# Two-block transformer kernel: first half of the gated features turned during the last read-out, last output units and router by tokens, activation tables loaded ahead

## What is computed

```python
def mlstm_readout(h, z, x_c, ml_norm, ml_skip):          # 4 heads of 256 features
    hf = h.transpose(0, 2, 1, 3)
    hn = hf * lax.rsqrt(jnp.mean(hf * hf, axis=-1, keepdims=True) + EPS)
    hn = hn.reshape(B, T, ML_INNER).astype(z.dtype) * ml_norm
    return jax.nn.sigmoid(z) * (hn + ml_skip * x_c)

def merge(y_mla, y_ml, g_mla, g_ml, w_out):
    return (jax.nn.sigmoid(g_mla) * y_mla + jax.nn.sigmoid(g_ml) * y_ml) @ w_out

def ec_moe(x, w_router, w_e_gate, w_e_up, w_e_down):     # 16 experts, 32 tokens each
    aff = jax.nn.softmax((x @ w_router).astype(jnp.float32), axis=-1)
    g, idx = lax.top_k(aff.transpose(0, 2, 1), cap)
    xs = jax.vmap(lambda xb, ib: xb[ib])(x, idx)
    a = jnp.einsum('becd,edf->becf', xs, w_e_gate)
    u = jnp.einsum('becd,edf->becf', xs, w_e_up)
    y = jnp.einsum('becf,efd->becd', jax.nn.silu(a) * u, w_e_down) * g[..., None].astype(x.dtype)
...
        x = x + g1[:, None, :] * out_l                    # out_l is what merge gives
        h_l = modulate(rmsnorm(x, norm2[l]), sh2, sc2)
        x = x + g2[:, None, :] * ec_moe(h_l, w_router[l], w_e_gate[l], w_e_up[l], w_e_down[l])
    return rmsnorm(x, final_norm)
```

## Time and profile before

| | us |
|---|---|
| runs: lowest, median, highest | 1703.22, 1708.28, 1709.57 |
| profiled execution: time | 1701.2 |
| profiled execution: span of the core | 1699.4 |
| busy in the span: PE, ACT, DVE, POOL | 1511.7, 525.2, 489.6, 601.3 |

### The profile page before, as it was taken

The page is one execution under the profiler, slowest core; times in us unless marked ns, Lnnn a source line. Parts: engine busy times, 40 slices in busy tenths (PEclk is TensorE's granted clock), DMA queues, the critical chain, the costliest instruction groups (busy, mean ns, idle before and its releaser), DMA issues.

```text
span 1699.4 us, 17483 instructions
## 1 busy us (share of the span) xinstructions
PE 1511.7 (89%) x7424; PEld 1010.9 (59%) x7424; DVE 489.6 (29%) x803; ACT 525.2 (31%) x683; POOL 601.3 (35%) x167
## 2 busy tenths in 40 slices
PE   5999999999999999999999999989887676676756
PEld 4776678877777658887788886657642131131111
DVE  2222333331222232332244346567410000000001
ACT  5255353433425524434344434254210000000000
POOL 4655187734655517774447671010000000000000
PEclk9999999999999999999999999889898898998898
DMA  6533355598453435569725443000799999999996
GB/s 239 185 124 125 124 176 179 183 334 292 157 178 111 147 125 175 177 198 380 252 91 174 149 138 96 1 15 1 299 405 423 421 421 421 422 421 422 422 422 285
DMA packets 125496, 395.38 MB, mean 233 GB/s; under 512 B 6743, under 2 KB 10644, under 8 KB 101228
## 3 DMA queue, kind: packets, MB, share of 16 engines
q1 hardware_dynamic: 123536, 388.66, 61.6%
q0 software_dynamic: 1456, 4.52, 0.7%
q10 hardware_dynamic: 428, 1.10, 0.2%
HBM read 393.19 MB, written 1.05 MB: 232 GB/s over the span
## 4 chain that ended last, share of the span: by engine, by line
PE 70%; DMA 23%; DVE 2%; ACT 2%; issue 1%; SPq 1%; ACTq 0%; DVEq 0%
PE psum L1960 16%; PE psum L1962 16%; PE psum L1961 16%; DMA ring<-in_w_e_down 6%; DMA arena<-in_w_e_gate 5%; DMA ring<-in_w_e_up 4%; PE psum L1952 4%; PE psum L1056 4%; DMA arena<-in_w_e_down 3%; DMA ring<-in_w_in 2%; DMA hT<-in_w_e_up 2%; DMA arena<-in_w_e_up 2%; PE psum L2191 1%; PE psum L973 1%; PE psum L844 1%
## 5 line engine op out<-in xcount | busy, mean ns | idle before, releaser
L593 POOL TENSOR_TENSOR ring_lo<-ring,ring_hi 128x2048 fp32r<-128x2048 f32 x101 | 467.8, 4636 | 362.2 <-ACT ring_hi L574 362.2
L1960 PE MATMUL psum<-ring_hi,hT_lo 128*128 128x512 f32 (+2 forms) x912 | 366.5, 402 | 16.1 <-DVE hT_lo L2209 10.6
L1962 PE MATMUL psum<-ring_hi,hT_hi 128*128 128x512 f32 (+2 forms) x912 | 356.8, 391 | 0.0
L1961 PE MATMUL psum<-ring_lo,hT_hi 128*128 128x512 f32 (+2 forms) x912 | 354.5, 389 | 0.0
L574 ACT ACTIVATE ring_hi<-ring 128x2048 fp32r<-128x2048 f32 x116 | 222.1, 1915 | 385.4 <-DMA ring<-in_w_in 123.0
L1056 PE MATMUL psum<-arena 128*32 128x512 f32 x740 | 169.6, 678 | 57.0 <-DMA arena<-in_w_e_gate 21.2
L1960 PEld LDWEIGHTS psum<-ring_hi,hT_lo 128*128 128x128 f32 x912 | 172.4, 189 | 58.6 <-issue 12.2
L1056 PE MATMUL psum<-ring,arena 128*32 128x512 f32 x708 | 156.6, 664 | 56.0 <-DMA ring<-in_w_e_down 19.9
L1962 PEld LDWEIGHTS psum<-ring_hi,hT_hi 128*128 128x128 f32 x912 | 172.1, 189 | 38.2
L1961 PEld LDWEIGHTS psum<-ring_lo,hT_hi 128*128 128x128 f32 x912 | 173.0, 190 | 33.9 <-issue 0.5
L1056 PEld LDWEIGHTS psum<-arena 128*32 128x32 f32 x740 | 36.0, 121 | 161.7 <-issue 55.9
(11 more groups left out here) (390 smaller groups left out, 1644.3 us busy)
## 6 DMA issues: line engine op xcount, KB each, us to landing
ring<-in_w_in SPq DMA_DIRECT2D x60, 1024.0 KB, 5.2
ring<-in_w_up SPq DMA_DIRECT2D x32, 1024.0 KB, 5.6
ring<-in_w_down SPq DMA_DIRECT2D x32, 1024.0 KB, 5.8
arena<-in_w_e_gate SPq DMA_DIRECT2D x31, 1024.0 KB, 26.7
arena<-in_w_e_up SPq DMA_DIRECT2D x31, 1024.0 KB, 27.0
ring<-in_w_e_gate SPq DMA_DIRECT2D x30, 1024.0 KB, 26.7
ring<-in_w_e_up SPq DMA_DIRECT2D x29, 1024.0 KB, 27.0
ring<-in_w_e_down SPq DMA_DIRECT2D x29, 1024.0 KB, 27.0
```

Source lines behind the costliest of these rows:

```text
L593: eng.tensor_tensor(slot_lo(u), slot(u), slot_hi(u).bitcast(F32), ALU.subtract).then_inc(done, 1)
L1960: pe.matmul(dst, lo(k0 + k), w_hi, start=start and k == 0, stop=False)
L1961: pe.matmul(dst, hi(k0 + k), w_lo, start=False, stop=False)
L1962: last = pe.matmul(dst, hi(k0 + k), w_hi, start=False, stop=stop and k == nk - 1)
```

## The change

All of it lies in the last part of the mixer and in the router.

- Heads are normed in pairs. `head_means` for heads 0 and 1 stands in `weights(3)`, their Sqrt (with `root_soon`, an activation of one column that loads the table) behind ACT's last decays, `head_gates` for them ahead of head 2's denominators, `head_sums` and the low half ahead of head 3's denominators. Heads 2 and 3 follow head 3's features.
- PE turns features 0 to 511 between the two tiles of head 3's read-out, and the second half between the two tiles of `out_unit(1, 0)`. The low half of the first goes to a tile of its own, `gatedT_lo`, since the decays and values of head 3 are still in use where it lay.
- The last two output units run by token tiles: (tile 0, columns 0), (tile 0, columns 1), (tile 1, columns 0), turning of x for tile 0, (tile 1, columns 1). The third unit's slot comes back after three quarters of this, the fourth's at its end.
- The router's logits are made for each tile of tokens by eight matmuls of 16 columns, 128 x 128 features each; part sums, their copy and the two summing matmuls are gone. `lg_full` 2 now says that the logits are done.
- `exp_ahead`, an activation of one column, loads the Exp table behind the root of the means; ACT's two scalings of x move behind the router's Exp. The first MAX8 and MATCH_REPLACE8 read PSUM, and the copy ahead of them is gone.

```diff
@@ PE
+                    if h == MH - 1 and t == 1:
+                        pe.wait_ge(mix_v, 8)
+                        turn_gated(0, 0)
...
-            pe.wait_ge(mix_v, 10)
-            turn_gated(0, 0)
+            def gated_rest():
+                pe.wait_ge(mix_v, 16)
+                turn_gated(1, 3)
+
             pe.wait_ge(gb_sb, 1)
             pe.wait_ge(turn_lo, 18 * DEPTH + 1)
             out_unit(0, 0)
-            pe.wait_ge(mix_v, 16)
-            turn_gated(1, 3)
-            out_unit(1, 0)
+            pe.wait_ge(h_v, 8 * MH)
+            out_unit(1, 0, gated_rest)
+            router_bias()
             pe.wait_ge(turn_lo, 18 * DEPTH + 2)
-            router_bias()
-            out_unit(0, 1)
-            out_unit(1, 1)
...
+            def turn_token(t, db):
+                for half in range(2):
+                    for k in range(4 * half, 4 * half + 4):
+                        last = pe.transpose(flat[db][:, k * P:(k + 1) * P], eighths(x[:, t, :], k), ident)
+                    last.then_inc(turn_full, 1)
+
+            def logits(t, half):
+                for k in range(4 * half, 4 * half + 4):
+                    last = pe.matmul(psum[:, t, 0:NE], hT[:, k, t * P:(t + 1) * P], wr[:, k, 0:NE], start=k == 0, stop=k == KC - 1)
+                return last
+
+            for t, n in ((0, 0), (0, 1), (1, 0), (1, 1)):
+                u = U_OUT + 2 + n
+                if t == 0:
+                    unit_ready(u)
+                if t and n:
+                    pe.wait_ge(x2_v, 4)
+                    pe.wait_ge(rt_v, 2)
+                    turn_token(0, 0)
+                last = split_product(DB[1 + n][:, t, :], tokens(hT_hi, t), tokens(hT_lo, t), UC, u, start=False, stop=True)
+                last.then_inc(slots_free if t else o2_half, 1)
+
+            pe.wait_ge(turn_a, TURN_A + 10)
+            logits(0, 0)
+            logits(0, 1)
+            pe.wait_ge(x2_v, 8)
+            turn_token(1, 3)
+            pe.wait_ge(turn_a, TURN_A + 11)
+            logits(1, 0)
+            pe.wait_ge(turn_v, TURN_V + 10)
+            logits(1, 1).then_inc(lg_full, 1)
@@ DVE
                 low_out(h)
+                if h == MH - 1:
+                    head_means(slice(0, 4), 4)
                 dve.wait_ge(raw_full, 2 * h + 2)
...
+                if h == MH - 2:
+                    head_gates(0, 5, 2)
                 if h == MH - 1:
-                    head_out(0, 3, 0, 6)
+                    head_sums(0, 6)
+                    dve.wait_ge(turn_a, TURN_A + 9)
+                    low_gated(0, flat[0])
                 dve.wait_ge(num_full, h + 1)
...
-            dve.wait_ge(lg_full, 4)
-            top_step(dve.tensor_copy(affT, psum[0:NE, 0, 0:T]))
+            dve.wait_ge(lg_full, 3)
             for r in range(CAP // 8):
                 eight = slice(8 * r, 8 * r + 8)
-                top_step(dve.max(top[:, eight], affT))
-                top_step(dve.match_replace(affT, top[:, eight], affT, -1.0))
+                left = affT if r else psum[0:NE, 0, 0:T]
+                top_step(dve.max(top[:, eight], left))
+                top_step(dve.match_replace(affT, top[:, eight], left, -1.0))
@@ ACT
                 if h == MH - 1:
+                    act.activation(root_soon, amp1[:, 0, 0:1], ACT.Sqrt).then_inc(at_sb, 1)
+                    act.wait_ge(mix_v, 1)
+                    act.activation(hst[:, 2, 0:4], hst[:, 1, 0:4], ACT.Sqrt).then_inc(hn_a, 1)
                     act.wait_ge(gb_full, 1)
...
             act.activation(half_r, means2, ACT.Sqrt).then_inc(norm_a, 1)
+            act.activation(exp_ahead, amp1[:, 0, 0:1], ACT.Exp).then_inc(at_sb, 1)
+            act.wait_ge(rt_v, 5)
+            for t in range(TT):
+                act.activation(aff[:, t, :], aff[:, t, :], ACT.Exp, bias=rst[:, 0, t:t + 1],
+                               accum_out=rst[:, 1, t:t + 1]).then_inc(rt_a, 1)
             act.wait_ge(norm_v, NORM_V + 3)
             for t in range(TT):
                 act.activation(xn[:, t, :], x[:, t, :], ACT.Copy, scale=r_sq[:, t:t + 1]).then_inc(norm_a, 1)
-            act.wait_ge(rt_v, 6)
```

More of the change, by code:

```diff
@@ L425, in build @@
         aff = piece(612, TT, NE)
-        root_ahead, table_ahead = piece(692, 1), piece(693, 1)
+        root_ahead, table_ahead, exp_ahead, root_soon = [piece(692 + i, 1) for i in range(4)]
         rst = piece(644, 4, TT)
@@ L952, in spread, with turn_gated @@
                 last.then_inc(gb_full, 1)
+            def turn_gated(half, db):
+                for k in range(4):
+                    for t in range(TT):
+                        c = 4 * half + k
+                        last = pe.transpose(flat[db][:, k * T + t * P:k * T + (t + 1) * P], gated[:, t, c * P:(c + 1) * P], ident)
+                last.then_inc(turn_full, 1)
             for h in range(MH):
@@ L975, in tensor_block2, with out_unit @@
                 last.then_inc(num_full, 1)
[L977 to L984, removed]
+            def out_unit(n, kh, between=None):
                 u = U_OUT + 2 * kh + n
@@ L987, in out_unit @@
                 for t in range(TT):
-                    last = split_product(DB[1 + n][:, t, :], tokens(hT_hi, t), tokens(hT_lo, t), UC * kh, u, start=kh == 0, stop=kh == 1)
+                    if t == 1 and between:
+                        between()
+                    last = split_product(DB[1 + n][:, t, :], tokens(hT_hi, t), tokens((gatedT_lo, hT_lo)[kh], t), UC * kh, u, start=kh == 0, stop=kh == 1)
                     if n == 1 and kh == 1 and t == 0:
@@ L1021, in tensor_block2 @@
-            pe.wait_ge(rt_v, 2)
-            for half in range(2):
-                if half == 0:
-                    pe.wait_ge(turn_v, TURN_V + 10)
-                else:
-                    pe.wait_ge(turn_a, TURN_A + 10)
-                for j in range(4):
-                    k = 4 * half + j
-                    last = pe.matmul(psum[32 * j:32 * j + 32, 0, 0:T], wr[:, k, :], hT[:, k, :], start=half == 0, stop=half == 1)
-            last.then_inc(lg_full, 1)
-            pe.wait_ge(rt_v, 3)
@@ L1032, in tensor_block2 @@
-            for t in range(TT):
-                last = pe.matmul(psum[:, 1, t * NE:(t + 1) * NE], part_sums[:, t * P:(t + 1) * P], const("sum16"), start=True, stop=True)
-            last.then_inc(lg_full, 1)
-            pe.wait_ge(rt_v, 9)
+            def turn_token(t, db):
+                for half in range(2):
+                    for k in range(4 * half, 4 * half + 4):
+                        last = pe.transpose(flat[db][:, k * P:(k + 1) * P], eighths(x[:, t, :], k), ident)
+                    last.then_inc(turn_full, 1)
@@ L1764, in scalar_block2 @@
                     squares_of(act, h - 1)
-            act.wait_ge(mix_v, 1)
-            act.activation(hst[:, 2, 0:6], hst[:, 1, 0:6], ACT.Sqrt).then_inc(hn_a, 1)
             act.wait_ge(turn_full, FULL + 5)
@@ L1783, in scalar_block2 @@
                 act.activation(xn[:, t, :], x[:, t, :], ACT.Copy, scale=r_sq[:, t:t + 1]).then_inc(norm_a, 1)
-            act.wait_ge(rt_v, 6)
-            for t in range(TT):
-                act.activation(aff[:, t, :], aff[:, t, :], ACT.Exp, bias=rst[:, 0, t:t + 1],
-                               accum_out=rst[:, 1, t:t + 1]).then_inc(rt_a, 1)
             act.wait_ge(gb_full, 2)
```

110 lines of the change are left out of this document (55 added, 55 removed).

## The result

| | us |
|---|---|
| changed kernel: lowest, median, highest of 11 | 1690.49, 1693.16, 1700.35 |
| kernel before: lowest, median, highest of 11 | 1702.53, 1706.84, 1710.68 |
| ratio, 95% interval | 0.9937 (0.9924 to 0.9951) |
| changed kernel, profiled execution: time, span | 1697.58, 1695.8 |

The change makes the kernel 0.63% faster, 10.7 us, with 8.4 to 13.0 as the interval; the two medians of the table lie further apart, 13.7.

The account below looks back on a forecast made before the run. The expert weight stream, limited only by DMA, was taken to bound the end: min(7.0 + 1.67, 8.9) = 8.67, less 0.2 for the dent, 8.5 us off the median 1708.28, giving 1699.8 us, range 1693.0 to 1704.5.

Parts of the forecast that it names:

- Two moments: Start of the expert weight stream: the end moves by the smaller of A's shift + 1.67 and B's shift.
- B: First issue into a slot that an expert round has given back, at 1244.33 us in the kernel before.
- A: First issue of an expert unit, when out_unit(0,0) gives its slots back, at 1200.48 us in the kernel before.
- A's shift: First expert issue from 1200.48 to 1193.5: 7.0 us earlier, 4.3 from waits and 2.7 from the clock.
- The margins: Slack at new waits: 0.85 us and 0.7 us in head 3's read-out, 0.6 us in out_unit(1,0).
- Rival 2: New waits on DVE bite and the clock falls at the output matmuls: gain 4 to 6 us, 1703.3; chance 0.12.
- rival 4: TensorE stays at 1.2 GHz through the output stage, making the kernel slower: 1718 us; chance 0.03.
- The Exp table: Router: table loaded ahead behind the root of the means, Exp at 1218.85, 8.6 us earlier.
- B's shift: First issue into a freed expert slot 8.9 us earlier: 8.6 from Exp, plus 0.45, less 0.1.
- A + 1.67: Gain allowed by the first expert issue: 7.0 plus 1.67 us lost in the stream's dent, 8.67, taken as binding.
- rival 1: B binds: a first expert round at the lower clock costs up to 1.9 us more, time 1701.3; chance 0.2.
- no window under 400 GB/s: Sign expected in the next profile: no such slow window of the expert stream around 1236 us.

Follow-up runs that it names:

- e4: Changed kernel, but the first four expert units (and units 8 and 9) wait for the second output unit, not the first; ratio to the kernel before 0.9973.
- e10: Changed kernel plus unread matmuls behind the gate row's spreading, the turning of the places and the first gathering; ratio to the kernel before 0.9937.
- e3: Kernel before plus output units by tokens, new logits, Exp table ahead and top-8 from PSUM, heads as before; ratio to the kernel before 0.9985.
- e6: Changed kernel plus five unread matmuls, two behind the logits and three behind the gate row's spreading; ratio to the kernel before 0.9948.
- e7: Changed kernel with the first two expert units issued when the last raw scores are done, into other slots; ratio to the kernel before 0.9943.
- e5: Changed kernel without the one-column Exp that loads the table ahead, ScalarE's order kept; ratio to the kernel before 0.9947.
- e9: Changed kernel without the one-column Exp and with ScalarE's two scalings of x ahead of the router's Exp again; ratio to the kernel before 0.9950.
- e12: Kernel before, unchanged, profiled a second time; ratio to the kernel before 0.9997.
- e1: Changed kernel again, no edit, timed and profiled a second time; ratio to the kernel before 0.9944.
- e11: Changed kernel with the unread matmuls of e10 and the early first two expert units of e7; ratio to the kernel before 0.9922.
- e2: Kernel before plus only the pairing of heads, the turning inside read-out 3 and out_unit(1, 0), and root_soon; ratio to the kernel before 0.9940.
- e8: Changed kernel with the edits of e6 and e7 together; ratio to the kernel before 0.9941.

## Why the prediction was right, and where it was not

The time, 1693.16, lies at the very edge of the range (from 1693.0), 6.6 us below the forecast, and the likeliest class was "within 0.5%" where it is 0.63% faster. Direction and mechanism held. The timed gain is 10.7 us where 8.5 were forecast; the base also came out 1.4 us lower than the three runs that the forecast started from (median 1706.84 against 1708.28). The traces of the stretch give 7.95 or, over two profiles of each kernel, 8.8. That this is so near to 8.5 is partly luck, as the last two points say.

- **Two moments set the end: shown.** Ten of the profiles end 455.0 to 455.4 us behind B, though B lies anywhere from 67 to 77. The other four are e4 and e10, where A leads and the end lies 497.8 and 497.3 behind it; e3, 455.41 behind B; and e6, 455.77, which stays unexplained. e4 and e7 moved A with B held, and the end moved with it only where A was the later side.
- **A's shift, 7.0: right (7.28).** Read-out 3 began 0.2 late, not 0.41 (DVE's reciprocal and scalings ended sooner). Transposes 0.88 against 0.89. First output matmul 4.86 earlier against 4.34, then 5.92 against 5.7 to A. The clock there was 1.00, as hoped.
- **The margins held.** No wait in the middle of read-out 3, nor before the second turning. Rival 2 did not happen, and rival 4 neither: from the second half of read-out 3 to 1214 the granted clock was 1.00.
- **Router.** Last sum 6.42 earlier against 6.25, logits used 7.70 against 7.85, Exp 8.44 against 8.6, MAX8 8.89 against 9.05, first expert round 8.98 against 8.9. MAX8 out of PSUM takes 0.42, as from SBUF.
- **The Exp table: right number, wrong reason.** The prediction needed the one-column Exp for the load to be ready. e5 and e9 show that the load does not wait for the Exp's data and that only the order of the scalings mattered (2.0 us). The Trainium skill's 2.66 us for a switch of tables (ScalarE: Activation LUTs, What ACT_TABLE_LOAD costs) is again not what the rows show: in e5 the root ends at 1220.01 and the load runs from 1220.03 to 1221.31; in e9 it ends at 1226.13 and the Exp starts at 1226.14. Nothing more stands between; the load alone, 1.28 us, is as the page has it (about 1283 ns).
- **The step that failed: B's last term.** The sum took B's shift as that of the round's start (8.9) and let A + 1.67 bind at 8.67, with 0.2 off. B came 8.01 earlier, because its first round took 5.93 us where the sum had left it at 4.96: B bound, not A + 1.67. That is rival 1, of moderate size, and it makes the stretch worth 7.95 between the two first profiles. The sign "no window under 400 GB/s" failed with it: the dent was 334, less deep than the 246 of before.
- **And the base was a lucky one.** The same term has a second side that the prediction left out. The duration of the first round differs between executions of one program, 4.96 and 6.59 us in the two profiles of before. It was 5.0 to 6.6 us in all profiles whose PE was not kept busy, and the first profile of before had the shortest. In the changed kernel and in e4, e5 and e7, which leave its PE work alone, it was 5.4 to 6.0. The term 1.67, read from the first profile, was right for it and not typical: end less A less the 497.3 to 497.8 us of an undisturbed stream gives 1.1 to 1.6 there and 3.1 to 3.6 in e12. With the two profiles of each kernel B's shift is 8.8 us, close to the 8.9 of the prediction, and so is the gain of the stretch, inside the interval of the ratio. The bound that the prediction chose instead, A + 1.67, gave nearly the same number by luck. Two profiles of a kernel are few for such an average. Whether the rest up to 10.7 is more of this or differences in the 1170 us in front is not settled; e1's session gave 9.5 (6.3 to 12.8).

## To carry to other kernels

Where a long transfer ends a kernel, the start of the transfer and the first buffer given back are two separate moments, and only the later one pays; find out which it is by moving one alone before working on either. Align two traces at the last instruction in front of the change before comparing them, and take a second profile of the kernel before: a term that depends on where the clock rises or falls differs between executions of the same program, and one trace shows one of its values. In these traces an activation table load goes ahead by itself when the scalar engine is free; what keeps it back is work that stands in front of it.

## What the runs showed of the hardware

The same gap can cost nothing or over two microseconds. Far in front of the change, PE waits some 3.3 us at 441 for the same data in both kernels. Before, 0.50 us is what the first matmul took after it, and the next ones start every 0.24 us; in the changed kernel's trace the clock has fallen, and they start every 0.43:

```profile
441.30 0.50 PE L1960 MATMUL psum<-ring_hi,hT_lo 128*128 128x512 f32 x1 [3.24 <-DVE hT_lo L2209]
441.63 0.40 PE L1961 MATMUL psum<-ring_lo,hT_hi 128*128 128x512 f32 x1
441.87 0.40 PE L1962 MATMUL psum<-ring_hi,hT_hi 128*128 128x512 f32 x1
```

```profile
441.47 0.80 PE L1990 MATMUL psum<-ring_hi,hT_lo 128*128 128x512 f32 x1 [3.28 <-DVE hT_lo L2239]
442.06 0.63 PE L1991 MATMUL psum<-ring_lo,hT_hi 128*128 128x512 f32 x1
442.49 0.63 PE L1992 MATMUL psum<-ring_hi,hT_hi 128*128 128x512 f32 x1
```

Four places account for most of where R began in the 14 profiles. This is the granted clock in the 15 or 20 us around each:

| | 160 to 175 | 440 to 455 | 580 to 600 | 1060 to 1080 | R |
|---|---|---|---|---|---|
| before, e12 | 1.00 | 1.00 | 1.00 | 0.74 | 1168.5, 1168.2 |
| e4 | 1.00 | 1.00 | 1.00 | 0.91 | 1168.5 |
| e11 | 0.89 | 1.00 | 1.00 | 1.00 | 1167.4 |
| e2, e3 | 0.89 | 1.00 | 1.00 | 0.74 | 1170.1, 1170.2 |
| e8 | 1.00 | 0.77 | 0.91 | 1.00 | 1169.9 |
| e10 | 0.89 | 0.89 | 1.00 | 0.83 | 1170.8 |
| e5 | 1.00 | 0.89 | 0.91 | 0.74 | 1171.3 |
| e6 | 1.00 | 0.77 | 0.91 | 0.83 | 1172.1 |
| changed | 1.00 | 0.77 | 0.91 | 0.74 | 1172.9 |
| e7, e1, e9 | 0.89 | 0.89 | 0.91 | 0.74 | 1172.9, 1173.1, 1173.7 |

The table loads of ScalarE show where the 4.35 us of the two first spans lie. The one at 97.68 in the kernel before comes at 97.90 in the changed one, the next, at 454.11, at 457.03, and the one at 909.05 at 913.64. So some 2.7 us went behind the gap at 441, and 1.7 between the last two loads, where the only fall of the clock is the one near 590. Two such falls are worth as much as half of the change. What comes behind the four places counts too: e4's load that stands at 1125.42 in the kernel before comes at 1122.78, but its R is no earlier. The last of the four places shows that PE need not stand still first: in 1060 to 1080 it was busy for all 20.00 us in the changed kernel and in e8, at granted clocks of 0.74 and 1.00.

Busy is also not always enough. In e6 and e8 PE had matmuls to do behind the last output matmuls without a gap over 0.3 us, and the clock still fell to 0.50, behind the router's 24 transposes and small matmuls of 16 columns. It stood at 1.00 for the first rounds of e10 and e11 after matmuls had filled most of the gaps in front of them, and fell again, to 0.50, for e10's second round and not for e11's, with the same matmuls in front of both.
